# Laying out a decoder kernel's weights and small inputs on the host, so that each transfer is one run per partition

## The reference, cut to what matters

```python
mod = c @ w_ada + b_ada                      # 9 rows of c; shift, scale, gate for two sub-layers
h = rmsnorm(x, norm1_w) * (1 + scale) + shift
z = h @ w_in                                 # conv inputs, q/k/v, indexer q/k/weights, two gates
y_a = (b_gate * conv3(c_gate * xin)) @ w_conv_out
y_b = sparse_attention(top-k keys by indexer; prompt keys, or 1024 cached keys in pages) @ w_attn_out
x = x + gate1 * ((sigmoid(g_a) * y_a + sigmoid(g_b) * y_b) @ w_out)
h2 = rmsnorm(x, norm2_w) * (1 + scale2) + shift2
q = h2 @ peer_w_q                            # product keys: 128 experts for each token
y = sum over the 128 of gate * gelu(u[e] . h2) * v[e]
return x + gate2 * y
```

## Time and profile before

| | us |
|---|---|
| median of 3 runs | 1128.17 |
| lowest and highest | 1127.29, 1130.02 |
| profiled execution | 1129.88 |
| its span, first to last instruction | 1128.1 |
| TensorE busy | 976.7 (87%) |
| VectorE busy | 717.7 (64%) |
| mean rate of the DMA engines | 337 GB/s |

### The profile page before, as it was taken

One profiled execution on the slowest core, in us unless ns is written; L12 is line 12 of the kernel. 1 busy time (PEld: TensorE's weight loads), 2 busy tenths in 40 slices (PEclk: granted clock), 3 DMA queues, 4 the chain that ended last, 5 costly groups with the idle time before them and its releaser, 6 DMA issues.

```text
span 1128.1 us, 11298 instructions
## 1 busy us (share of the span) xinstructions
PE 976.7 (87%) x3389; PEld 500.0 (44%) x3389; DVE 717.7 (64%) x1731; ACT 393.0 (35%) x1129; POOL 303.3 (27%) x330
## 2 busy tenths in 40 slices
PE   6998889999999899999998777787778877887777
PEld 3446667676677755554443222232222222222222
DVE  1457466888655678676888788886445444454544
ACT  2111223213412344444455344334333333333333
POOL 0111001002000224344333333333333333333330
PEclk9999889999999999999999999999999999999999
DMA  9962423868456699999999999999999999999994
GB/s 310 356 218 77 137 93 108 283 219 293 124 188 236 231 363 412 419 420 419 420 418 421 419 422 418 420 420 420 419 421 419 421 420 420 419 422 418 422 419 165
DMA packets 81936, 379.91 MB, mean 337 GB/s; under 512 B 7004, under 2 KB 16472, under 8 KB 45012
## 3 DMA queue, kind: packets, MB, share of 16 engines
q0 software_dynamic: 44736, 312.90, 68.1%
q1 hardware_dynamic: 36966, 66.19, 17.0%
q10 hardware_dynamic: 174, 0.11, 0.0%
HBM read 377.59 MB, written 1.59 MB: 336 GB/s over the span
## 4 chain that ended last, share of the span: by engine, by line
DMA 44%; PE 41%; DVE 8%; ACT 4%; issue 2%; SPq 0%; POOL 0%; DVEq 0%; ACTq 0%; POOLq 0%
DMA big<-peer_uv,oT 39%; PE twoA L580 8%; PE twoD L953 6%; PE twoD L955 6%; PE twoA L893 5%; PE twoD L834 3%; DVE big L1815 2%; PE twoA L558 2%; DMA r<-peer_uv,oT 2%; PE twoA L503 2%; DMA big<-w_in 1%; PE twoD L822 1%; PE twoA L734 1%; ACT big L1299 1%; PE twoD L640 1%
## 5 line engine op out<-in xcount | busy, mean ns | idle before, releaser
L1071 POOL DMA_INDIRECT big<-peer_uv,oT x259 | 246.3, 951 | 497.2 <-PE twoD L955 383.3
L953 PE MATMUL twoD<-big 128*128 128x512 f32 x518 | 286.5, 635 | 104.3 <-ACT big L1299 104.0
L1815 DVE CUSTOM_DVE_ANT_0 big<-big,twoA 128x1024 f32<-128x1024 f32 x145 | 177.0, 1221 | 165.9 <-DMA big<-peer_uv,oT 165.0
L955 PE MATMUL twoD<-big 128*128 128x512 f32 x518 | 265.6, 594 | 0.0
L953 PEld LDWEIGHTS twoD<-big 128*128 128x128 f32 x518 | 82.2, 189 | 285.0 <-ACT big L1299 260.1
L1294 ACT ACTIVATE oT<-oT 128x1 f32<-128x1 f32 x288 | 58.3, 203 | 382.5 <-DVE oT L1815 380.4
L1815 DVE CUSTOM_DVE_ANT_0 big<-big,twoD 128x1024 f32<-128x1024 f32 x114 | 138.9, 1219 | 53.4 <-DMA big<-peer_uv,oT 51.9
L955 PEld LDWEIGHTS twoD<-big 128*128 128x128 f32 x518 | 99.0, 191 | 125.0 <-issue 125.0
L1299 ACT ACTIVATE big<-ctab,oT 128x128 f32<-128x128 f32 x288 | 115.6, 401 | 9.5
L580 PE MATMUL twoA<-hT,big 128*128 128x288 f32 x448 | 117.5, 419 | 0.0
L580 PEld LDWEIGHTS twoA<-hT,big 128*128 128x128 f32 x448 | 86.1, 196 | 28.8 <-issue 5.9
(11 more groups left out here) (333 smaller groups left out, 947.3 us busy)
## 6 DMA issues: line engine op xcount, KB each, us to landing
big<-w_ada SPq DMA_DIRECT2D x12, 2048.0 KB, 8.4
big<-w_in SPq DMA_DIRECT2D x5, 2048.0 KB, 13.4
big<-w_in SPq DMA_DIRECT2D x9, 1024.0 KB, 7.8
big<-peer_w_q SPq DMA_DIRECT2D x3, 2048.0 KB, 8.8
big<-peer_uv,oT POOLq DMA_INDIRECT x259, 22.9
big<-w_out SPq DMA_DIRECT2D x2, 2048.0 KB, 11.8
big<-w_conv_out SPq DMA_DIRECT2D x1, 2048.0 KB, 14.0
big<-w_attn_out SPq DMA_DIRECT2D x2, 1024.0 KB, 17.3
```

The source lines that it names most:

```text
L953: pe.matmul(acc[0][:, :], diag[j % NDG], row[:, 0:512], start=(s == 0), stop=(s == SLOTS[t] - 1), skip_group_check=True)
L955: mm = pe.matmul(acc[1][:, :], diag[j % NDG], row[:, 512:D], start=(s == 0), stop=(s == SLOTS[t] - 1), skip_group_check=True)
L1071: pool.indirect_dma_start(pairs[home[i]], None, peer_uv, bass.IndirectOffsetOnAxis(ap=eidx[:, t, s:s + 1], axis=0)).then_inc(row_in[home[i ...
L1815: dve.tensor_tensor_reduce(out=row, in0=row, in1=h2tok[t][:, :], scale=1.0, scalar=0.0, op0=ALU.mult, op1=ALU.add, accum_out=dots[:, t, s: ...
```

## The change

The host now builds three more tables. `weight_rows` holds all weights in the order in which the kernel loads them: row p holds, group after group, what partition p gets, so that a 512-column group is one run of 16 KB for each partition (8 KB for a gate group, 10.25 KB for `kvw`, 16 KB for `convout` and `attnout`). A row of the table is 485,632 bytes long. `front_rows` holds c (turned and padded with zeros), the small vectors (turned), the conv state (turned) and the q/k norm weights repeated on all partitions: 524 values, or 2,096 bytes, for a partition. `token_rows` holds the tokens turned: 2,304 values, or 9,216 bytes, for a partition.

In the kernel every group is one transfer from `weight_rows`. SyncE's queue begins at once with the first group of weights. The constants' first columns and the tokens move to ScalarE's queue, which now has three transfers: `front_rows`, constants, tokens. TensorE's turning of tokens, c and small vectors is gone, and so are VectorE's memset of `cT` and its twelve copies. ScalarE waits once for `in_x` ahead of the eight squares, instead of for each copy. The order of the weight groups, their slots and their waits are as before.

```diff
+PLAN = [("ada", 2, 0), ("ada", 3, 1), ("ada", 0, 5), ("ada", 1, 6), ("q", 0, 0), ("kvw", 0, 1), ("qi", 0, 5),
+        ("conv", 0, 6), ("conv", 1, 0), ("conv", 2, 1), ("ada", 4, 5), ("gate", 0, 2), ("gate", 1, 3), ("ada", 5, 6),
...
+    return np.concatenate([columns(name, i).reshape(SHAPE[name][0], P, -1).transpose(1, 0, 2).reshape(P, -1)
+                           for name, i, _ in PLAN], axis=1)
...
+    return np.ascontiguousarray(x.reshape(TOK, DC, P).transpose(2, 1, 0).reshape(P, DC * TOK))
...
-            pe.wait_ge(in_ident, 16)
-            pe.wait_ge(consts_ready, 4)
-            pe.wait_ge(in_c, 16 * 2)
-            b = V.open(pe)
-            for c in range(DC):
-                mm = pe.transpose(b[:, 9 * c:9 * c + 9], crow[0:9, c * P:(c + 1) * P], ident[0:9, 0:9])
-            V.close(mm)
-            pe.wait_ge(in_x, 48)
-            for c in range(DC):
-                b = V.open(pe)
-                for t in range(3):
-                    mm = pe.transpose(b[:, COLS[t]:COLS[t] + ROWS[t]], xin[0:ROWS[t], t, c * P:(c + 1) * P],
-                                      ident[0:ROWS[t], 0:ROWS[t]])
-                V.close(mm)
...
+            pe.wait_ge(in_front, 16)
...
-            pe.wait_ge(cT_ready, 1)
             first_part(0)
+            pe.wait_ge(consts_ready, 4)
             sum_bank.append(bankA[3])
             for c in range(DC):
                 square_sum(c, 0)
             first_part(1)
+            pe.wait_ge(in_ident, 16)
             ada_turn(adarow)
...
         def _(sp):
-            sp.dma_start(ctab[:, 0:CONST_FIRST], consts[:, 0:CONST_FIRST]).then_inc(in_ident, 16)
-            for t in range(2):
-                sp.dma_start(xin[:, t, :], x_prompt[t * P:(t + 1) * P, :]).then_inc(in_x, 16)
-            sp.dma_start(xin[0:NSM, 2, :], x_sample).then_inc(in_x, 16)
...
-                    for src, _, width in what:
-                        sp.dma_start(dst[:, :, at:at + width], src).then_inc(w_landed[slot_of[g]], 16)
-                        at += width
+                k, n = SHAPE[name]
+                sp.dma_start(wring[slot_of[g]][:, 0:k * n], weight_rows[:, row_at[g]:row_at[g + 1]]).then_inc(w_landed[slot_of[g]], 16)
...
+            act.dma_start(fronts[:, :], front_rows).then_inc(in_front, 16)
+            act.dma_start(ctab[:, 0:CONST_FIRST], consts[:, 0:CONST_FIRST]).then_inc(in_ident, 16)
+            act.dma_start(xT[:, :, :].rearrange("p c t -> p (c t)"), token_rows).then_inc(in_x, 16)
...
+            act.wait_ge(in_x, 16)
             for c in range(DC):
-                act.wait_ge(xT_ready, c + 1)
                 L.tell(act.activation(sq[:, c * TOK:(c + 1) * TOK], xT[:, c, :], ACT.Square), sq_ready)
```

More of the change, by code:

```diff
@@ new lines, with weight_table, columns @@
+SHAPE = {"ada": (DC, 512), "adaG": (DC, 512), "q": (DC, 512), "kvw": (DC, 328), "qi": (DC, 512), "conv": (DC, 512),
+         "gate": (DC, 256), "convout": (CC, D), "attnout": (NG, D), "out": (DC, 512), "peerq": (DC, 512)}
+FRONT_PARTS = [("cT", DC * 32), ("small", 76), ("state", CC * NB * 2), ("qk", 2 * HD)]
+def weight_table(w):
+    def columns(name, i):
+        if name in ("ada", "adaG"):
+            return w["w_ada"][0][:, 512 * i:512 * i + 512]
+        if name == "kvw":
+            return np.concatenate([w["w_in"][0][:, C_K:C_K + 256], w["w_in"][0][:, C_KI:C_KI + 72]], axis=1)
+        if name == "attnout":
+            return w["w_attn_out"][0].reshape(NKV, NG, HD, D).transpose(1, 0, 2, 3).reshape(NG * P, D)
+        first, n = {"q": (C_Q, 0), "qi": (C_QI, 0), "conv": (0, 512), "gate": (C_GA, 256)}.get(name, (0, 512))
+        of = {"convout": "w_conv_out", "out": "w_out", "peerq": "peer_w_q"}.get(name, "w_in")
+        return w[of][0][:, first + n * i:first + n * i + SHAPE[name][1]]
+    return np.concatenate([columns(name, i).reshape(SHAPE[name][0], P, -1).transpose(1, 0, 2).reshape(P, -1)
+                           for name, i, _ in PLAN], axis=1)
@@ new lines, in front_table, with turned @@
+def front_table(a):
+    def turned(rows):
+        return rows.reshape(rows.shape[0], -1, P).transpose(2, 1, 0)
+    c = np.zeros((P, DC, 32), np.float32)
+    c[:, :, 0:9] = turned(np.concatenate([a["c_prompt"], a["c_sample"]], axis=0))
+    small = [a[n][0].reshape(-1, P).T for n in ("b_ada", "norm1_w", "norm2_w", "conv_w")]
+    state = turned(a["state_conv"][0].reshape(NB * 2, CONV)).reshape(P, -1)
+    qk = np.tile(np.concatenate([a["q_norm_w"][0], a["k_norm_w"][0]])[None, :], (P, 1))
+    return np.concatenate([c.reshape(P, -1)] + small + [state, qk], axis=1)
@@ L171, in layer_program @@
         ones = sb("ones", [P, P])
-        smallT = sb("smallT", [P, 76])
-        qkw = sb("qkw", [P, P])
-        cT = sb("cT", [P, DC, 32])
+        fronts = sb("fronts", [P, sum(w for _, w in FRONT_PARTS)])
+        fv, at = {}, 0
+        for n, w in FRONT_PARTS:
+            fv[n] = fronts[:, at:at + w]
+            at += w
+        cT = fv["cT"].rearrange("p (c b) -> p c b", b=32)
+        smallT, qkw = fv["small"], fv["qk"]
+        stateT = fv["state"].rearrange("p (c b) -> p c b", b=NB * 2)
         modT = sb("modT", [P, 48, 9])
@@ L358, in layer_program @@
             sem("acc_done"), sem("acc_taken"), sem("y_ready"))
[L361 to L389, removed]
+        FIRST_ADA = [i for name, i, _ in PLAN if name == "ada"][0:4]
+        names = [name for name, _, _ in PLAN]
+        slot_of = [slot for _, _, slot in PLAN]
+        row_at = [0]
+        for name in names:
+            row_at.append(row_at[-1] + SHAPE[name][0] * SHAPE[name][1])
         shares = {0: (0, 2, 3), 1: (1,), 2: (0, 2), 3: (0, 3), 4: (4,), 5: (5,), 6: (6,)}
@@ L398, in weights @@
         def weights(eng, g):
-            eng.wait_ge(w_landed[slot_of[g]], 16 * sum(len(groups[j][1]) for j in range(g + 1) if slot_of[j] == slot_of[g]))
-            k, n = groups[g][1][0][1], sum(part[2] for part in groups[g][1])
-            n = D if names[g] == "attnout" else n
+            eng.wait_ge(w_landed[slot_of[g]], 16 * sum(1 for j in range(g + 1) if slot_of[j] == slot_of[g]))
+            k, n = SHAPE[names[g]]
             return wring[slot_of[g]][:, 0:k * n].rearrange("p (k n) -> p k n", n=n)
@@ L567, in _ @@
             blocks = iter([(gg, j) for gg, name in enumerate(names) if name in ("conv", "gate")
-                           for j in range(groups[gg][1][0][2] // P)])
+                           for j in range(SHAPE[name][1] // P)])
             def fill(n):
@@ L966, in _ @@
         def _(sp):
-            sp.dma_start(ctab[:, 0:CONST_FIRST], consts[:, 0:CONST_FIRST]).then_inc(in_ident, 16)
-            for t in range(2):
-                sp.dma_start(xin[:, t, :], x_prompt[t * P:(t + 1) * P, :]).then_inc(in_x, 16)
-            sp.dma_start(xin[0:NSM, 2, :], x_sample).then_inc(in_x, 16)
-            for g, (name, what) in enumerate(groups):
+            for g, name in enumerate(names):
                 if slot_of[g] == 4:
@@ L1365, in _ @@
             dve.wait_ge(consts_ready, 4)
[L1366 to L1372 removed]
+            dve.wait_ge(in_front, 16)
+            dve.wait_ge(in_x, 16)
             def bias(a, e, turned):
```

72 lines of the change are left out of this document (17 added, 55 removed).

## The result

| | before | changed |
|---|---|---|
| median of 6 runs each | 1130.33 us | 1133.77 us |
| lowest and highest | 1127.29, 1131.95 | 1133.07, 1136.12 |
| ratio, with 95% interval | | 1.0033 (1.0017 to 1.005) |
| profiled execution's span | 1128.1 us | 1131.2 us |

The changed kernel is 3.4 us slower by the medians, 0.3%: small, but the interval does not include 1. The forecast was 3.9 us slower (1132.1 against a median of 1128.17). A second timing of the unaltered changed kernel, in a later call, gave 1.0016 (1.0002 to 1.0029). Two executions of some 1.94 ms among all those timed, one of the kernel before and one of the run with the late page table, are left out of every ratio.

What follows compares the result with a forecast made beforehand. The prediction took expert gathers as the bound, passing head delays on whole. Late tokens and TensorE's low clock moved w_ada's fourth part from 35.1 to 39.0 us: +3.9, 1132.1 us against the median 1128.17, range 1124.3 to 1134.2.

Steps and rivals of the forecast that it cites:

- What bounds the kernel: Expert gathers bound the later stage; delays before the first gather pass on whole; weight speed matters only in the head.
- The size: Whole kernel: w_ada's fourth part ends at 39.0 instead of 35.1 us, so 3.9 us slower, 1132.1 us against the median.
- Rate of long runs: Head's weight transfers: 420 GB/s instead of 387, 0.62 us per 16 KB packet; fourth part of w_ada lands at 29.5 us.
- The half microsecond for the semaphore: Fourth part of w_ada: 0.5 us added after its bytes land at 29, giving 29.5 us.
- Turns by the packet: SyncE's and ScalarE's queues alternate packet by packet, so `in_x` comes at 24.2 us instead of 10.3; chance 0.52.
- The clock: TensorE's squares' sum after the idle stretch: low clock for 5.4 us (3.4 to 6.7), then 1.2 us more.
- S: End of the squares' sum on TensorE: 27.0 us before, forecast 31.3; the fourth part of w_ada ends 7.7 us later.
- The later stages, costed at nothing: Weight transfers after the head add 0 us; if their cover failed, about 4 us would fall on the chain once.
- the prediction's own sign: Timelines before and after: if the distance at 45 us is not that at 380, a cover of the middle failed.
- Shares by bytes: Rival for the head's queues: they share by bytes, `in_x` at 12.7 us, gain 2.0 to 3.7 us, 1125.2 us; chance 0.30.
- Slow 16 KB packets: Rival for head weights: 200 to 250 GB/s, fourth part lands 7 to 14 us later, 1139 us; chance 0.05.
- Tokens near the turning point: Rival for the head: `in_x` near 20 us, where gain and loss meet (20.4), no change, 1128 us; chance 0.11.

Runs made afterwards that it cites:

- the late page table: Changed kernel with tokens at the head of SyncE's queue and GpSimd asking for the page table after w_ada's fourth part landed; 1126.09 us, ratio 0.9961 to the kernel before.
- the tokens first: Changed kernel with the tokens' transfer at the head of SyncE's queue instead of third on ScalarE's; 1128.31 us, ratio 0.9981 to the kernel before.
- 4 KB packets: Changed kernel with each of the first four weight groups sent as four transfers of 4 KB a partition; 1128.67 us, ratio 0.9985 to the kernel before.
- the squares first: Changed kernel with tokens at the head of SyncE's queue and the squares' products ahead of w_ada's first part on TensorE; 1126.8 us, ratio 0.9975.
- long runs alone: Kernel before with only the host table of weights, one transfer a group; tokens, c and small vectors still turned by TensorE; 1128.74 us, ratio 0.9985.
- 2 KB runs: Changed kernel with the weight table keeping 512-column groups as eight 2 KB runs a partition, tokens still on ScalarE's queue; 1131.53 us, ratio 1.0013.
- all orders changed: Changed kernel with tokens first on SyncE's queue, constants ahead of `front_rows`, squares before w_ada's first part, page table after the q columns; 1122.61 us, ratio 0.994.
- all orders with added work: The run with all orders changed plus unread TensorE products, three before the squares and one before the q columns; 1124.47 us, ratio 0.9948.

## Why the prediction was right, step by step

*What bounds the kernel.* Right to a microsecond or two: the stage of the gathers took 747.5 us before and 748.3 and 745.8 in the two profiles of the changed kernel. A delay in the head reached the first gather in the main: 2.8 us at the q product and 2.3 at the first gather in the one profile, 3.5 and 2.2 in the other.

*The size.* That 3.9 us were forecast and 3.4 measured is in part luck. The heads gave 2.8 and 3.5 us, the spans of the same two profiles 3.1 and 0.5, and the medians of the two timings 3.4 and 2.4. The head's delay is shown; the last microsecond or two of the total is not shown to come from the change.

*Rate of long runs.* 420 GB/s taken, 420 to 439 measured, by window. The bound from the instruction fetches (1.3 us for 16 KB) does not hold for weights: the shares above make it 64.5% x 16 x 6 us / 104 = 0.60 us for one packet, where 0.62 was taken. The landing of the fourth part with nothing in its way was put at 29.5 us, and it began at 28.70 with the tokens first, where it waited for its weights. The half microsecond for the semaphore in that 29.5 has no row behind it, and the sum of +3.9 does not use it.

*Turns by the packet.* Right, and the step that decided: `in_x` was expected at 24.2 us, and the first square began at 23.95. Taken from two queues of other issuers with 4 and 8 KB packets, the rule held for 16 KB; and the runs with 4 KB packets and with eight times the tokens' packets confirm it at 12.6 and 35.3 us, where the same sum gave 13.2 and 36. The Trainium skill's rule (DMA: Bandwidth & Descriptors, Queues, rings and completion order) agrees with 104 packets against 102. A packet is here one run of 16 KB or 9 KB (1.65 MB in 104 and 0.91 MB in 102).

*The clock.* The mechanism was right and the term at the upper end: 1 us too dear in the first profile, right in the second. The squares' sum was to take 6.6 us and took 5.84, for the low level held until about 28, 3.5 us after the sum began, not 5.4. S came at 30.4 instead of 31.3, the end of the fourth part at 37.9 instead of 39.0: +2.8 us in place of +3.9. From S to the end passed 7.5 us, 7.7 taken. In the second profile the sum took 6.51 us and ended at 31.1, and the fourth part ended at 38.66, +3.5. The range of 3.4 to 6.7 us at the low level had room for both.

*The later stages, costed at nothing.* Almost right. From 50 us to the first gather TensorE waits for no transfer, in the kernel before and in both profiles of the changed one. By the prediction's own sign (another distance at 380 us than at 45) something in the middle did move, by 0.5 and 1.3 us in the two profiles. The profiles differ in between by several microseconds without a cause in the transfers: with the tokens first and with the squares first the q product ends at 36.5 alike, yet 48 products of 288 columns begin at 160.5 in the one and 163.9 us in the other. Some 2.4 us of this come from 16 products, here first with the tokens first, then with the squares first:

```profile
129.73 4.05 PE L575 MATMUL twoA<-hT,big 128*128 128x288 f32 x16
```

```profile
130.22 6.41 PE L575 MATMUL twoA<-hT,big 128*128 128x288 f32 x16
```

The granted clock around them is 1.00 in the one and 0.63 in the other. These are stretches in which the granted clock falls or not, like those of the earlier trace rows. Over the twelve timed runs with the tokens first, the device time goes from 1124.0 us at a mean clock of 0.992 to 1130.2 at 0.983, about 0.7 us for each 0.001. Their clock is 0.9868 on average, that of the kernel before in the same call 0.9883. An estimate from these is that 1 us of the 2.5 us by which the median's gain (2.0) falls short of the head's (4.5) is clock; that the profile is of the fastest execution may be more of it, and the rest is not accounted for. This is why I read the mechanism from the heads of the traces and only the sign from the ratios. What decides the clock in those stretches was not tried.

*A stall that no step foresaw.* In most profiles with the host table, the kernel before with long runs alone included, TensorE loses 0.8 to 1.7 us within the indexer's products, with a gap put down to "issue": the profile shows nothing that it waits for. The line of the kernel before and the two of the kernel with long runs alone, at the same instructions:

```profile
193.67 1.93 PE L683 MATMUL twoA<-r,qkbuf 128*32 128x256 f32 x32
```

```profile
192.87 1.64 PE L685 MATMUL twoA<-r,qkbuf 128*32 128x256 f32 x10
194.81 1.52 PE L685 MATMUL twoA<-r,qkbuf 128*32 128x256 f32 x22 [0.30 <-issue]
```

32 products take 1.93 us in the one; in the other 10 take 1.64 us, then comes a gap, and 22 take 1.52. It is there with 2 KB runs too, so long packets are not its cause. It is in the first profile of the changed kernel and not in the second:

```profile
197.37 1.93 PE L678 MATMUL twoA<-r,qkbuf 128*32 128x256 f32 x32
```

So it comes and goes in one and the same kernel, as it is absent in both profiles with all orders changed. With one profile of the kernel before it is not shown that the host table brings it; the cause stays open.

*Rivals.* Shares by bytes is refuted by the changed kernel's own queue shares and by the tokens in eight transfers. Slow 16 KB packets are refuted by 427 GB/s. Tokens near the turning point did not happen as changed. The two runs that brought the tokens in at 12.5 and 12.6 us had heads that ended 0.7 and 1.4 us earlier than before, which is the right side of a turning point at 20.4; where it lies was not tried.

## What to carry to other kernels

When a transfer moves to another queue, count packets and not bytes: as long as the neighbour has work, it lands after as many of the neighbour's packets as it has of its own on an engine, so making the neighbour's packets longer delays it even while the total rate rises. Put what the compute chain needs first at the head of the queue that has the long packets, and look for a second wait on the same queue (here the constants) before counting on it. A gain in a data-bound head is real only to the point where the next transfer or TensorE's clock becomes the bound: look at the end of the stage, not at the instruction that moved.

## What the runs showed of the hardware that was not expected

The page table's broadcast, 32 KB in 16 packets, holds all 16 engines for 1.5 to 2 us: its queue has 16.0% of their time from 2 to 12 us with the tokens first, 1.6 us, and without it beside them the first 2 MB of weights land at 11.9 us instead of 14.1. Asked for later, it took time from the q columns instead.

A low clock of TensorE goes with waits for data in the head. The fourth part of w_ada, 16 products, took 1.92 us where TensorE had waited up to 0.7 us for it (the kernel before, tokens first, late page table), and 3.31 to 3.64 us where it had waited 1.1 to 3.6 us (4 KB packets, 2 KB runs, all orders with added work). With all orders changed the third part took 3.06 us after a wait of 2.1 us, and the fourth 3.21 without one, though the second, after 1.1 us, took 1.92. The waits were not varied by themselves. In the runs with the late page table and with all orders changed, these low stretches stood where the earlier weights should have paid, and the q product ended at 36.5 and 36.6 us, as with the tokens first alone.
